# A decoder layer on one core: queries and two gate projections as seven-product couples ahead of the values, and a conv stage of two tiles a turn

## The reference, cut to what matters

```python
h = rmsnorm(x, norm_pre1) * (1 + sc1[:, None]) + sh1[:, None]
bg, cg, ua, q, k, v, r, lr, ga, gb = jnp.split(h @ w_in, split_idx, axis=-1)
y_a = bg * causal_dwconv(cg * ua, conv_buf, conv_w, conv_b)
o, gla_state_new = gla_recurrence(q * DK ** -0.5, k, v, log_a, gla_state)
merged = sigmoid(ga) * y_a + sigmoid(gb) * rmsnorm(o, gla_norm) * silu(r)
x = x + g1[:, None] * rmsnorm(merged @ w_out, norm_post1)
```

## Time and profile before

| | us |
|---|---|
| median of 3 runs (lowest, highest) | 980.48 (980.03, 981.25) |
| the profiled execution | 982.61 |
| its span in the profile | 980.9 |
| PE matmul busy in the span | 963.1 |
| DVE / ACT / POOL busy | 564.9 / 434.2 / 222.4 |
| granted TensorE clock, mean | 0.998 |
| HBM read and written | 107.02 MB and 7.35 MB, 117 GB/s |

### The profile page before, as it was taken

How to read it: one execution, slowest core, us unless ns; L and a number is a source line. 1 busy time by engine, 2 the same in 40 slices (tenths; PEclk the granted TensorE clock), 3 DMA queues, 4 the chain that set the end, 5 groups by cost and what they waited for, 6 DMA issues and landing times.

```text
span 980.9 us, 18498 instructions
## 1 busy us (share of the span) xinstructions
PE 963.1 (98%) x7599; PEld 875.2 (89%) x7599; DVE 564.9 (58%) x842; ACT 434.2 (44%) x692; POOL 222.4 (23%) x121
## 2 busy tenths in 40 slices
PE   5999999999999999999999999999999999999997
PEld 4889888989999999999898889999999999888886
DVE  2511205476565655345348589998999988660204
ACT  4535333134343324444444365655565556633212
POOL 3033532243333333333254000000000000013430
PEclk9999999999999999999999999999999999999999
DMA  9676353798466657545438023133323332422212
GB/s 330 229 103 190 108 86 87 156 97 150 147 144 165 141 131 139 67 137 152 102 120 242 1 84 88 46 107 99 96 87 95 100 97 75 121 74 86 87 52 96
DMA packets 145028, 115.58 MB, mean 118 GB/s; under 512 B 11225, under 2 KB 121585, under 8 KB 144945
## 3 DMA queue, kind: packets, MB, share of 16 engines
q1 hardware_dynamic: 144849, 114.38, 46.5%
q10 hardware_dynamic: 96, 0.04, 0.0%
HBM read 107.02 MB, written 7.35 MB: 117 GB/s over the span
## 4 chain that ended last, share of the span: by engine, by line
PE 95%; DVE 2%; ACT 1%; issue 1%; DMA 1%; SPq 0%; DVEq 0%; ACTq 0%
PE pair L2150 39%; PE pair L2567 20%; PE pair L2256 17%; PE pair L2524 5%; PE pair L2140 2%; PE pair L2337 1%; PE pair L2310 1%; PE pair L2080 1%; DMA x_tok<-in_x_prompt 1%; PE pair L2248 1%; PE pair L2400 1%; PE pair L2389 1%; PE pair L2249 1%; PE pair L2250 1%; PE pair L2247 1%
## 5 line engine op out<-in xcount | busy, mean ns | idle before, releaser
L933 POOL TENSOR_TENSOR w_lo<-raw,w_hi 128x1024 fp32r<-128x1024 f32 x53 | 129.2, 2439 | 537.6 <-ACT w_hi L1007 537.6
L2150 PE MATMUL pair<-h_hi,w_hi 128*128 128x288 f32 x944 | 213.7, 302 | 0.1
L2150 PE MATMUL pair<-h_hi,w_lo 128*128 128x288 f32 x944 | 207.4, 296 | 0.9 <-issue 0.9
L2150 PE MATMUL pair<-h_lo,w_hi 128*128 128x288 f32 x944 | 206.8, 295 | 0.0
L2150 PEld LDWEIGHTS pair<-h_hi,w_hi 128*128 128x128 f32 x944 | 153.2, 189 | 18.4 <-issue 16.7
L2150 PEld LDWEIGHTS pair<-h_hi,w_lo 128*128 128x128 f32 x944 | 153.5, 188 | 1.1 <-issue 1.1
L2150 PEld LDWEIGHTS pair<-h_lo,w_hi 128*128 128x128 f32 x944 | 153.4, 188 | 0.0
L1007 ACT ACTIVATE w_hi<-raw 128x1024 fp32r<-128x1024 f32 x66 | 69.6, 1057 | 161.7 <-PE pair L2250 80.2
L933 POOL TENSOR_TENSOR w_lo<-raw_c,w_hi 128x1024 fp32r<-128x1024 f32 x24 | 69.1, 2883 | 125.3 <-ACT w_hi L1007 125.3
L2567 PE MATMUL pair<-t_hi,w_hi 128*128 128x288 f32 x304 | 90.1, 296 | 0.7 <-ACT u_buf L1282 0.7
L2567 PE MATMUL pair<-t_lo,w_hi 128*128 128x288 f32 x304 | 89.7, 295 | 0.0
(11 more groups left out here) (361 smaller groups left out, 1751.3 us busy)
## 6 DMA issues: line engine op xcount, KB each, us to landing
raw_c<-in_w_ada SPq DMA_DIRECT2D x32, 512.0 KB, 5.1
raw<-in_w_in SPq DMA_DIRECT2D x224, 64.0 KB, 3.2
raw_c<-in_w_in SPq DMA_DIRECT2D x192, 64.0 KB, 3.7
raw<-in_w_up SPq DMA_DIRECT2D x24, 512.0 KB, 3.8
raw<-in_w_down SPq DMA_DIRECT2D x22, 512.0 KB, 3.7
raw_up<-in_w_up SPq DMA_DIRECT2D x20, 512.0 KB, 3.8
ada_first<-in_w_ada SPq DMA_DIRECT2D x16, 512.0 KB, 9.6
raw<-in_w_in SPq DMA_DIRECT2D x8, 512.0 KB, 4.8
```

Source lines behind the costliest of these rows:

```text
L933: pool.tensor_tensor(lo, raw_tile(n)[:, :], hi.bitcast(F32), ALU.subtract).then_inc(S("w_lo_done"), 1)
L2150: ins = pe.matmul(bank[pair][:, half, 0:HALF], w[:, i, :], x[:, i, HALF * half:HALF * half + HALF], start=i == 0 and p == 0, stop=i == KT ...
```

## The change

- `EARLY` = 10 couples (c = 0 to 9) stand behind the four key tiles and ahead of the values: c = 0, 1 give the four query tiles, c = 2 to 9 give sigmoid(ga) and bg of channel block c - 2. Each is seven products of 12 matmuls (`early_products`). Factors of the activations (`th_32`, `th_hi`, `th_lo`) are made once. DVE makes the sums and all low parts of these tiles, POOL none; ACT makes the high parts. y_a is filled with sigmoid(ga) * bg here (`early_gate`), with no conv yet.
- The raw tiles of the couples go in turn to raw[0], raw[1] and raw_c[2], raw_c[3], a couple's loads waiting for the couple before last. The first loads for the values and for conv tiles 2 and 3 wait for lows of couples 8 and 9; ada block 0 waits for all of y_a.
- The copies of the sample columns (`h_smp_hl`), before behind the first query tile, stand on ACT behind the high part of the third value tile. Clearing the scores and the copies of the conv parameters move on DVE too.
- The conv stage keeps eight turns, with two tiles each (cg, ua). An item or another piece stands between the two halves (`part`) of a tile, where before it stood behind a whole tile: items at e = 0, 2, 4 as before, `mod_back` at e = 6, and both ada pairs at e = 7. Four ada blocks are loaded together in each turn, a pair ahead of each tile's load.
- The first tap, the history columns and the tails move from DVE to ACT (`mix_first_tap`, `mix_history`, `mix_tails`). On DVE the order of a turn is: items, qd and kd, conv input, suffix, two taps, prefix, `take_mod`, two multiplications of y_a by the conv, the copy of the ada rows. ACT has no sigmoid in this stage any more.
- Counters of later stages are shifted by the new instructions (`SUMS_0`, `C_SUMS_0`, `A_DONE_0`).

```diff
-TILE_K, TILE_Q, TILE_V = 0, HEADS, 2 * HEADS
+EARLY = HEADS // 2 + KT
+TILE_K, TILE_E, TILE_V = 0, HEADS, HEADS + 4 * EARLY
 TILE_C1 = TILE_V + 8
-TILE_C2 = TILE_C1 + 4 * KT
+TILE_C2 = TILE_C1 + 2 * KT
 TILE_WO = TILE_C2 + 2 * KT
...
+    th_32 = [place(f"th_32_{i}", [P, 4, HALF], offset=g_at + at_) for i, at_ in enumerate((0, 4608, 60928, 88064))]
+    th_hi = [place(f"th_hi{i}", [P, 4, HALF], F32R, offset=x_at + 4608 * i) for i in range(4)]
+    th_lo = [place(f"th_lo{i}", [P, 4, HALF], F32R, offset=g_at + 36864 + 4608 * i) for i in range(4)]
+    es12 = place("es12", [P, 1024], offset=g_at + 55296)
+    eu1 = place("eu1", [P, HALF], offset=g_at + 59392)
+    eu2 = place("eu2", [P, HALF], offset=g_at + 65536)
+    ep5 = place("ep5", [P, HALF], offset=g_at + 66688)
+    ec22 = place("ec22", [P, HALF], offset=g_at + 67840)
+    sga = place("sga", [P, T], offset=g_at + 92672)
...
-            return 0
-        if n in (4, 5):
-            return 2
+            return early_fill(EARLY - 1, n - TILE_C1) + 1
+        if TILE_V <= n < TILE_V + 2:
+            return early_fill(EARLY - 2, n - TILE_V + 2) + 1
...
+    def level_products(dve, lv):
+
...
+        dve.tensor_tensor(dst, dst, src, ALU.mult).then_inc(S("qd_done"), 1)
+        if B > 1:
...
+            dve.wait_ge(S("kd_exp"), lv - 1)
+            dve.tensor_tensor(kd[:, :, 0:w], kd[:, :, 0:w], k[:, :, 0:w], ALU.mult).then_inc(S("kd_done"), 1)
+
+    def level_suffix(dve, lv):
+
+        dve.tensor_tensor(level_side(suf, lv, 0), level_side(suf, lv, 0), level_side(pre, lv, 1, True), ALU.add) \
+           .then_inc(S("suf_add"), 1)
+
+    def level_prefix(dve, lv):
+
+        dve.wait_ge(S("suf_add"), lv)
+        dve.tensor_tensor(level_side(pre, lv, 1), level_side(pre, lv, 1), level_side(pre, lv, 0, True), ALU.add) \
+           .then_inc(S("level_set"), 1)
...
+            def load_early(c, x):
+                if c < 2:
+                    cols = IN_Q + DK * (2 * c + x)
+                    sp.wait_ge(S("w_lo_done"), 2 * c + 2)
+                else:
+                    cols = (IN_GA, IN_BG)[x] + P * (c - 2)
+                    sp.wait_ge(S("w_lo_done"), early_fill(c - 2, 2 + x) + 1)
+                dst, src = kc(early_raw(c, x)), in_cols(cols)
+                for i in range(KT):
+                    sp.dma_start(dst[:, i, :], src[:, i, :]).then_inc(S(early_landed[c, x][0]), 16)
...
                 elif n < 6:
+                    if n == 2:
+                        sp.wait_ge(S("ya_done"), 2 * KT)
+                        sp.wait_ge(S("ring_free"), TILE_V)
                     load_ada(n - 2)
...
+            for i in range(4, 2 * KT + 4):
+                if i >= 6:
+                    load_ada(2 * i - 8)
+                    load_ada(2 * i - 7)
+                if i < 2 * KT:
+                    load_c1(TILE_C1 + i)
+                else:
+                    load_c2(i - 2 * KT)
...
+            pool.wait_ge(S("w_lo_done"), TILE_V)
+            with pool.Fori(TILE_V // 4, TILE_C1 // 4) as g:
...
+            high(3)
+            keys_out(0)
+            decay_abs(0)
+            factor_high(0)
+            factor_high(1)
+            keys_out(1)
+            keys_out(2)
+            early_high(0, 0)
+            factor_high(2)
+            factor_high(3)
+            early_high(0, 1)
+            keys_out(3)
+            early_u1(0)
+            early_high(0, 2)
+            early_high(0, 3)
+            decay_abs(1)
+            for c in range(EARLY):
+                n = c + 1
+                if n < EARLY:
+                    early_high(n, 0)
+                else:
+                    high(TILE_V)
+                early_u2(c)
+                early_p5(c)
+                if n < EARLY:
+                    early_high(n, 1)
+                else:
+                    high(TILE_V + 1)
+                if c >= 2:
+                    gate_sigmoid(c)
+                if n < EARLY:
+                    early_high(n, 2)
+                    early_u1(n)
+                    if c < 2:
+                        queries_out(c)
+                    early_high(n, 3)
+                    if c in (1, 2):
+                        decay_abs(c + 1)
+                else:
+                    high(TILE_V + 2)
+
+            act.wait_ge(S("ring_free"), TILE_V)
+            act.wait_ge(S("h_hi_done"), KT + 2)
+            act.wait_ge(S("h_lo_done"), KT)
+            act.activation(h_smp_hl[:, :, 0:64], h_hi[:, :, SEQ:T].bitcast(F32), ACT.Copy).then_inc(S("stacked"), 1)
...
+            def mix_first_tap(j):
+                act.wait_ge(S("u_done"), 3 * j + 3)
+                act.wait_ge(S("hist"), j + 1)
+                act.wait_ge(S("ya_done"), 2 * KT + 2 * j)
+                tap, b = CW + 16 + j, CB + j
+                act.activation(cv[:, :], ext[:, 2:EXT], ACT.Identity, bias=prm[:, b:b + 1], scale=prm[:, tap:tap + 1]) \
+                   .then_inc(S("conv"), 1)
...
                 high(n + 4)
-                high(n + 5)
                 if j + 1 < KT:
                     qd_exp(act, j + 1)
+                    if j > 0:
+                        kd_exp(act, j + 1)
                 else:
 
                     act.wait_ge(S("level_set"), KT)
                     act.activation(suf[:, :, :], suf[:, :, :], ACT.Exp, scale=TAU_INV).then_inc(S("exps"), 1)
+                mix_first_tap(j)
+                mix_tails(j)
...
+            for c in range(EARLY):
+                n = c + 1
+                early_c11(c)
+                early_low(c, 3)
+                if n < EARLY:
+                    early_sums12(n)
+                    early_low(n, 0)
+                if c in (1, 2, 3):
+                    decay_min(c)
+                early_c22(c)
+                if n < EARLY:
+                    early_low(n, 1)
+                early_c12(c)
+                if n < EARLY:
+                    early_sums34(n)
+                if c >= 2:
+                    early_gate(c)
+                if n < EARLY:
+                    early_low(n, 2)
...
+            for j in range(KT):
+                for e in (0, 2, 4):
+                    for i in after_tile(j, e):
+                        take_item(dve, i)
                 if j + 1 < KT:
-                    dve_level(dve, j + 1)
-                else:
-
+                    level_products(dve, j + 1)
+                else:
                     dve.wait_ge(S("exps"), 1)
                     dve.tensor_tensor(k[:, :, :], k[:, :, :], suf[:, :, :], ALU.mult).then_inc(S("decayed"), 1)
-                    dve.wait_ge(S("exps"), 2)
-                    dve.tensor_tensor(q[:, :, :], q[:, :, :], pre[:, :, :], ALU.mult).then_inc(S("decayed"), 1)
+                conv_input(j)
                 for i in after_tile(j, 6):
                     take_item(dve, i)
+                if j + 1 < KT:
+                    level_suffix(dve, j + 1)
+                mix_taps(j)
+                if j + 1 < KT:
+                    level_prefix(dve, j + 1)
                 if j > 0:
                     take_mod(dve, j - 1)
-                dve.wait_ge(S("t_done"), 3 * (j + 1))
-                dve.wait_ge(S("sga_done"), j + 1)
-                dve.tensor_tensor(y_a[:, j, :], y_a[:, j, :], buf_b[:, :], ALU.mult).then_inc(S("ya_done"), 1)
+                conv_gate(j)
                 for i in after_tile(j, 7):
                     take_item(dve, i)
-
                 dve.wait_ge(S("ada_mm"), 2 * (j + 1))
                 if j > 0:
                     dve.wait_ge(S("back"), j)
                 dve.tensor_copy(rows_ada[:, :], one_bank(6)[:, :]).then_inc(S("rows_ada"), 1)
+            dve.wait_ge(S("exps"), 2)
...
+            def early_products(c):
+                b11, b21, b22 = (quarters(h_hi, h_lo, k, t) for k, t in ((0, 0), (1, 0), (1, 1)))
+                t1, t2, t3, t4 = ((th_hi[i][:, :, :], th_lo[i][:, :, :]) for i in range(4))
+                a, b, cc, d = ((w_hi[i], w_lo[i]) for i in range(4))
+                x, y, z = 2 + c % 2, 4, 5
+
+                def factors_made(n):
+                    if c == 0:
+                        pe.wait_ge(S("h_lo_done"), KT + n)
+
+                pe.wait_ge(S("w_lo_done"), early_fill(c, 0) + 1)
+                if c < 2:
+                    pe.wait_ge(S("kq_done"), 2)
+                elif c < 4:
+                    pe.wait_ge(S("kq_done"), HEADS + 3 * (c - 1))
+                else:
+                    pe.wait_ge(S("ya_done"), 2 * (c - 3))
+                block_product(a, 0, b11, x, True).then_inc(S("x_mm"), 1)
+                if c == 0:
+                    pe.wait_ge(S("kq_done"), 3)
+                else:
+                    pe.wait_ge(S("c_sum"), 3 * c - 2)
+                block_product(a, 1, b21, y, True).then_inc(S("ring_free"), 1)
+                pe.wait_ge(S("w_lo_done"), early_fill(c, 1) + 1)
+                pe.wait_ge(S("a_done"), 3 * c + 1)
+                factors_made(1)
+                block_product(b, 1, t2, x, False).then_inc(S("x_mm"), 1)
+                if c > 0:
```

(42 more changed lines are left out.)

402 lines of the change are left out of this document (246 added, 156 removed).

## The result

The changed kernel takes 1016.2 us (median of 4 runs, 1014.3 to 1017.6) against 980.5 in the same comparison: ratio 1.036, 95% interval 1.034 to 1.038. The forecast was 987, range 971 to 997: the sign was right, the size far off. The profiled execution took 1016.0 us for a span of 1014.3, against 982.6 and 980.9, so the difference to explain is +33.4 us of span.

A forecast was written before the change was run, and what follows sets the result against it. PE, busy 963.1 of 980.9 us, was taken as the bound, with what makes it wait. Terms -16.0 + 1.5 + 17.7 - 0.9 + 2.7 + 1.3 = +6.3 gave 988.9 profiled, 987 median; range 971 to 997.

The forecast's parts named there:

- The matmuls: Twenty tiles of 48 matmuls become ten couples of 84: 120 fewer at 0.133 us each, -16.0 us.
- The level loop: Conv turns: PE waits for take_mod, queued on DVE behind the level, prefix slowed by POOL's low; +17.7, bounds 6.3 and 21.
- The take into turn 1: Conv stage: PE waits for the fifth item's take, behind the gate; 2.3 us, or 0.5 without POOL.
- The clock: Matmuls were costed at 0.133 us each; the forecast held 0 for a lower clock in conv stage, couples and V entry.
- Transfers: Conv turn loads of 3.15 MB: 0 at 240 GB/s, the faster row; at 124 a turn takes 25.4 us.
- Rival 3: DMA queue becomes the bound in the conv stage: 998 for two slow turns, 1032 through the stage; chance 0.11.
- SP's order: Conv turn: at 240 GB/s the last ada block lands by 11 of the 15 us it has, cost 0.
- V entry: V tile 0: PE waits after 12 matmuls for ACT's sample-column copies behind V tile 2's high; +2.7, bounds 0 and 5.
- First couple: Couple 0: product 7 waits for c22, which stands on DVE behind sums and couple 1's first low; +1.3, bounds 0 and 3.
- Restarts: Conv stage: tiles cut by items; a start behind something else costs 0.18 more, one more a turn; +1.5 in all.
- Rival 1: Same loop, POOL's lows beside copies or PSUM readers: 6.3 instead of 17.7, -5.1 in all, 975; chance 0.21.
- rival 2: PE stays the bound everywhere, the loop being shorter than counted: -16.0 + 1.5 = 966; chance 0.12.

The follow-up runs named there:

- run 10: On run 9: one DMA a tile in the couples, couple 5's tiles in a buffer of their own, couple 7 following couple 3 in its buffer; 967.9 us, ratio 0.986.
- run 2: Changed kernel, with ACT's high of tile n+3 moved behind the history copy, which waits for the taps; 1004.1 us, ratio 1.025.
- run 3: Changed kernel, with h_smp_hl in a place of its own and ACT making its two copies in couple 6; 1009.0 us, ratio 1.029.
- run 5: Changed kernel, with PE making 12 to 34 identity transposes ahead of the first score item of turns 1 to 7; 1011.7 us, ratio 1.032.
- run 6: Changed kernel, with couples 2 to 9 loading ga and bg columns four tiles further on, output left wrong; 1015.0 us, ratio 1.035.
- run 9: Changed kernel with early take_mod, takes and sample copies, both highs of a turn together, and SP issuing a turn's tiles ahead of its adaLN blocks; 975.6 us, ratio 0.994.
- run 1: Changed kernel, with take_mod on DVE moved behind the conv input, ahead of suffix, taps and prefix; 999.1 us, ratio 1.019.

## Why the prediction was wrong

Point by point:

- **The matmuls** (-16.0): right, counted and shown by run 10.
- **The level loop** (+17.7): the step that set the sign was right in mechanism and nearly in size, 17.8 us on DVE mod. The stalls into turns 2 to 7 were to be 3.9, 3.9, 3.1, 1.6, 1.6 and 1.3 and are 4.4, 4.3, 3.5, 1.8, 1.9 and 1.8. The chain of 12.9 us and the prefix beside a POOL low came out, and so nearly did the 5.8 us on mod without that collision (run 2: 6.8). The take into turn 1 did not: 3.3 us for 2.3, and 3.4 without the collision for 0.5. Of the 17.7, 15.4 were for mod (17.8 measured) and 2.3 for the take into turn 1 (3.3 measured); together 21.1, at the upper bound of 21 that I gave.
- **The clock**: the step that failed. Every stall was costed at its own length, and the matmuls behind it at 0.133 us, since the rows that I had taken of before show the clock at 1.00; but before has almost no waits in these stages, so these rows could not show what follows one. Seven waits, some 27 us long together, brought 14.5 us on top of themselves (9.7 + 4.8). Run 3 shows 3.0 us for one wait of 4.2, run 5 that the clock stays up when the waits are filled.
- **Transfers** (0): "from the faster row, to which most of the stage is nearest" was wrong in kind. The slow rate belonged to certain columns, not to a share of the time; run 6 shows it for ga and bg, run 9 for cg and ua. I costed the couples' loads by SP's issue time alone, 7.6 of 11.2 us, and gave them no bound by the slow row: a couple's 1.05 MB at the 53 GB/s that the kernel after shows from 103 to 120 (busy share 1.00) is 20 us. That cost 5.6 us and the clock behind it. Rival 3 had the mechanism and the wrong stage.
- **SP's order**: the step named the blocks' landing against their need and not what stands behind them on SP. With both adaLN pairs at the end of a turn the blocks wait for PE longer, in front of tiles with free buffers. The stops called issue (3.1 us, 4.8 once the waits were out of the way) are PE's own instructions landing late; that the crowd behind SP's wait delays them is what run 9 speaks for.
- **V entry** (+2.7, measured 4.2): the chain came out in its order. PE was there 14.1 us from the start of couple 9 (14.2 by my count), and the copies ended at 18.3 (16.9 by my count); the clock's 3 us on top were missing.
- **First couple** (+1.3, measured 1.2): right. **Restarts** (+1.5): not seen; PE's busy time in the conv stage of run 10 is 0.4 us less than the count from before.
- **Rival 1** (no collision) and **rival 2** (PE stays the bound, 966) did not happen in the kernel as changed. Rival 2's 966 is what run 10 comes near (967.9), with DVE's, ACT's and SP's order altered and a buffer more.

A sign of the clock's fall stood in the trace of before, outside these stages. Behind a PE wait of 2.5 us at the start the granted clock is 0.54 (the second line, columns as in the earlier trace rows):

```profile
14.56 3.53 PE L2092 MATMUL pair<-ident,x_tok 128*128 128x128 f32 x16 [2.49 <-DVE x_tok L1475]
```
```profile
14.56:18.09 3.53, 3.52 (x18) 3.53 (x19) 2.59 (x4) 1.03 (x1) 0.00 (x0) 0.54 1.06 388
```

It shows that the clock can fall behind such a wait, but not the price: the kernel after took 3.67 us for the same 16 transposes at a clock of 1.00.

What should have widened the range: nearly all that I added were waits of 1 to 5 us at places where PE had not waited before, so one error common to all waits came back with each of them, and the bounds treated them as independent.

## What to carry to other kernels

A short instruction on which PE depends must not be queued behind a chain on which PE does not: list for every wait of PE what stands ahead of its releaser on that engine. The same holds for a DMA queue: a load that waits for compute goes behind the loads that could start already. And where PE is the bound, a wait of some us can cost more than its length (7.2 us for 4.2 in run 3); if it can't be removed, harmless matmuls in it give part of that back (4.5 us in run 5).

## What the runs showed of the hardware

- In the kernel after, the granted clock fell to its lower level at each of the six PE waits of 3.3 to 5.6 us in these stages (0.55 over the 6.6 us behind one of 3.3) and behind one of three of 1.84 to 1.85. It stayed at 1.00 when transposes filled the waits of the conv turns. A 4.2 us wait cost 7.2 in all. Between these lengths it went both ways: it fell behind 2.37 us in run 1 and 2.19 in run 2, and stayed up behind 2.60 in run 5 and 2.64 in run 6.
- Stretches that load tiles of w_in with the same shape and row distance show 96 GB/s (busy share 0.69) or 57 (0.93), by the columns loaded, and eight DMAs a tile or one made no difference.
- PE stopped for up to 5.5 us (run 5) in front of a matmul that waits for no other engine, and went on 1.2 to 1.5 us after a 16 KB piece of its instruction queue had landed. Loading tiles earlier took away the stop of 4.8 us and left one of 2.0.
- A two-operand DVE instruction of 64 columns, 0.21 us alone, took 2.40 beside a POOL low.
